# Query projections as pairs of high and low tokens in the two cross attentions of a fused two-block kernel, and four convolution taps in another place

## The reference

```
q = (h @ xq_w).reshape(B, S, 4, 256)                 # h is the normed stream
s = einsum('bshd,bmhd->bhsm', q, k) * 256 ** -0.5
o = einsum('bhsm,bmhd->bshd', softmax(s), v).reshape(B, S, 1024)
x = x + o @ xo_w
...
u = a * sigmoid(b)
y = conv_general_dilated(u, conv_w[:, None, :], padding=[(30, 0)], feature_group_count=512) + conv_b
```

## Time and profile before

| | |
|---|---|
| median of 3 runs | 913.3 us (912.95 to 915.75) |
| time of the profiled execution | 913.01 us |
| its span, first to last instruction | 910.9 us |
| mean granted TensorE clock | 0.999 |
| PE busy | 901.4 us, 99% |
| DVE busy | 661.6 us, 73% |
| ACT busy | 504.2 us, 55% |
| HBM read | 162.65 MB, 180 GB/s over the span |

### The profile page before, as it was taken

The page is one execution under the profiler, slowest core; times in us unless marked ns, Lnnn a source line. Parts: engine busy times, 40 slices in busy tenths (PEclk is TensorE's granted clock), DMA queues, the critical chain, the costliest instruction groups (busy, mean ns, idle before and its releaser), DMA issues.

```text
span 910.9 us, 12836 instructions
## 1 busy us (share of the span) xinstructions
PE 901.4 (99%) x5160; PEld 787.4 (86%) x5160; DVE 661.6 (73%) x920; ACT 504.2 (55%) x584; POOL 24.3 (3%) x69
## 2 busy tenths in 40 slices
PE   9999999999999999999999999999999999999997
PEld 8888998889888888888888988888899888888886
DVE  5799999987577666656967996646686676565665
ACT  6796435655555444445656757744464654544444
POOL 1600010000000000000000000000000000000000
PEclk9999999999999999999999999999999999999999
DMA  9746555454355666654755455455453456666551
GB/s 353 253 159 223 183 199 185 139 185 140 92 186 186 195 199 197 190 185 153 238 188 183 159 166 183 152 175 187 173 185 103 144 183 191 196 193 197 189 185 47
DMA packets 101280, 164.38 MB, mean 180 GB/s; under 512 B 2736, under 2 KB 71088, under 8 KB 101104
## 3 DMA queue, kind: packets, MB, share of 16 engines
q1 hardware_dynamic: 100528, 161.71, 54.2%
q0 software_dynamic: 560, 1.84, 0.7%
q10 hardware_dynamic: 144, 0.16, 0.1%
HBM read 162.65 MB, written 1.05 MB: 180 GB/s over the span
## 4 chain that ended last, share of the span: by engine, by line
PE 92%; DVE 5%; DMA 2%; ACT 1%; issue 1%; SPq 0%; DVEq 0%; ACTq 0%
PE ps L609 20%; PE ps L611 19%; PE ps L610 19%; PE ps L646 18%; PE ps L650 9%; DVE w_lo L1719 1%; DVE c_acc L1865 1%; DMA w_ring<-in_w_in 1%; PE ps L737 1%; DMA head_raw<-in_head 1%; PE ps L857 0%; ACT w_hi L1227 0%; PE ps L774 0%; DVE mem_l L1734 0%; PE ps L826 0%
## 5 line engine op out<-in xcount | busy, mean ns | idle before, releaser
L1719 DVE TENSOR_TENSOR w_lo<-w_ring,w_hi 128x2048 fp32r<-128x2048 f32 x146 | 333.4, 2288 | 114.2 <-ACT w_hi L1227 113.2
L1227 ACT ACTIVATE w_hi<-w_ring 128x2048 fp32r<-128x2048 f32 x146 | 278.6, 1911 | 88.3 <-DMA w_ring<-in_w_in 27.3
L646 PE MATMUL ps<-xx,w_hi 128*128 128x512 f32 x720 | 171.8, 391 | 0.3
L646 PEld LDWEIGHTS ps<-xx,w_hi 128*128 128x128 f32 x720 | 133.3, 188 | 27.4 <-issue 0.7
L609 PE MATMUL ps<-w_hi,xx 128*128 128x512 f32 x304 | 120.2, 395 | 0.0
L611 PE MATMUL ps<-w_hi,xx 128*128 128x512 f32 x304 | 118.6, 390 | 0.0
L610 PE MATMUL ps<-w_lo,xx 128*128 128x512 f32 x304 | 118.5, 390 | 0.0
L650 PEld LDWEIGHTS ps<-xx,w_lo 128*128 128x128 f32 x720 | 92.3, 191 | 3.5
L650 PE MATMUL ps<-xx,w_lo 128*128 128x256 f32 x720 | 93.4, 283 | 0.0
L609 PE MATMUL ps<-w_hi,ff_h 128*128 128x512 f32 (+1 forms) x218 | 84.7, 389 | 0.0
L610 PE MATMUL ps<-w_lo,ff_h 128*128 128x512 f32 (+1 forms) x218 | 84.6, 388 | 0.0
(11 more groups left out here) (339 smaller groups left out, 1335.9 us busy)
## 6 DMA issues: line engine op xcount, KB each, us to landing
w_ring<-in_w_in SPq DMA_DIRECT2D x34, 1024.0 KB, 5.1
w_ring<-in_mlp_up_w SPq DMA_DIRECT2D x16, 1024.0 KB, 5.6
w_ring<-in_mlp_down_w SPq DMA_DIRECT2D x16, 1024.0 KB, 4.9
w_ring<-in_w_gate_ffn SPq DMA_DIRECT2D x11, 1024.0 KB, 5.3
w_ring<-in_w_up_ffn SPq DMA_DIRECT2D x11, 1024.0 KB, 5.3
w_ring<-in_w_down_ffn SPq DMA_DIRECT2D x11, 1024.0 KB, 4.9
w_ring<-in_xkv_w SPq DMA_DIRECT2D x8, 1024.0 KB, 5.4
w_ring<-in_w_out SPq DMA_DIRECT2D x8, 1024.0 KB, 4.8
```

The source lines that it names most:

```text
L646: pe.matmul(feat(bank + b), wh[:, k, b * P:(b + 1) * P], xx[:, k, :, :].rearrange("p e t -> p (e t)"), start=k == 0, stop=False)
L1227: act.activation(w_hi[:, s, :], w_ring[:, s, :], ACT.Copy).then_inc(hi_done, 1)
L1719: dve.tensor_tensor(w_lo[:, s, :], w_ring[:, s, :], w_hi[:, s, :].bitcast(F32), ALU.subtract).then_inc(lo_done, 1)
```

## The change

In each attention the second and the third query slab (heads 1 and 2) are taken by `form_a_pair` in place of `form_a`: head 1 into banks 6 and 7, head 2 into banks 4 and 5. The fourth stays with `form_a` but goes into `feat(2)`, the first stays as it is. A new tile `q_s` (in the place of a part of `xn`) takes the sums: ACT copies the low tokens' halves there (`q_half`), DVE adds the high tokens' halves (`q_sum`), and only then `q(j)` and `q_lo(j)` read it. On ACT `q_half(1)` stands ahead of `q(1)` and `q_half(2)` ahead of `q(2)`. On DVE `q_sum(1)` takes the place of `q_lo(1)`, which moves behind `normalise(0)`; `q_sum(2)` stands ahead of `q_lo(2)`. The banks in which head 0, 1, 2 and 3 are turned and their values formed are `feat(3)`, `feat(0)`, `feat(1)` and `feat(2)` (`place`). In the convolution four of the 16 steps ahead of `lo(11)` move behind it, so that 8 stand between `lo(11)` and `lo(12)` in place of 4.

```diff
+        q_s = at("q_s", [P, 2, 2, S], xn0)
+        pair_banks = {1: ps[:, 6:8, :], 2: ps[:, 4:6, :]}
+        xq_half, xq_sum = sem("xq_half"), sem("xq_sum")
...
             def form_a_pair(i, bank, step=0, ready=(), low_ready=None):
+                banks = bank if type(bank) is tuple else (4 + bank, 5 + bank)
...
             def x_attention(b, i_q, i_o, ready, between):        # PE
+                place = (3, 0, 1, 2)
...
                 form_a(i_q, (0,), (xh, xl), 256, 0, *ready)
-                form_a(i_q + 1, (1,), (xh, xl))
+                form_a_pair(i_q + 1, 2)
                 scores(0)
-                form_a(i_q + 2, (2,), (xh, xl))
+                form_a_pair(i_q + 2, 0)
                 scores(1)
                 turn(0)
-                form_a(i_q + 3, (3,), (xh, xl))
+                form_a(i_q + 3, (2,), (xh, xl))
                 scores(2)
...
             def x_attention(b, i_q, i_o):                        # ACT
                 def q(j):
+                    if j in (1, 2):
+                        act.wait_ge(xq_sum, 2 * b + j)
+                        src = q_s[:, j - 1, :, :]
+                    else:
+                        used_slab(i_q + j)
+                        src = blocks(feat(2 if j else 0))
+                    act.activation(q_h[:, 2 * j:2 * j + 2, :], src, ACT.Copy).then_inc(xq_hi, 1)
+
+                def q_half(j):
+                    act.wait_ge(norm_sq, 2 * (Q_XA, Q_XA2)[b] + 2)
                     used_slab(i_q + j)
-                    act.activation(q_h[:, 2 * j:2 * j + 2, :], blocks(feat(j)), ACT.Copy).then_inc(xq_hi, 1)
+                    act.activation(q_s[:, j - 1, :, :], pair_banks[j][:, :, S:2 * S], ACT.Copy).then_inc(xq_half, 1)
...
                 q(0)
+                q_half(1)
                 q(1)
                 hi(i_o)
                 exps(0)
                 hi(i_o + 1)
+                q_half(2)
                 q(2)
                 p_t(0)
...
-            conv(16)
+            conv(12)
...
             lo(11)
-            conv(4)
+            conv(8)
             lo(12)
...
+                def q_sum(j):                                    # DVE
+                    dve.wait_ge(xq_half, 2 * b + j)
+                    q = q_s[:, j - 1, :, :]
+                    dve.tensor_tensor(q, pair_banks[j][:, :, 0:S], q, ALU.add).then_inc(xq_sum, 1)
...
                 q_lo(0)
                 if b == 0:
                     lo(I_Q1 + 3)
-                q_lo(1)
+                q_sum(1)
                 maxima(0)
                 normalise(0)
+                q_lo(1)
                 lo(i_o)
                 lo(i_o + 1)
+                q_sum(2)
                 q_lo(2)
                 p_lo(0)
```

More of the change, by code:

```diff
@@ L645, in form_a_pair @@
                     for b in range(2):
-                        pe.matmul(feat(bank + b), wh[:, k, b * P:(b + 1) * P], xx[:, k, :, :].rearrange("p e t -> p (e t)"), start=k == 0, stop=False)
+                        pe.matmul(ps[:, banks[b], :], wh[:, k, b * P:(b + 1) * P], xx[:, k, :, :].rearrange("p e t -> p (e t)"), start=k == 0, stop=False)
                 pe.wait_ge(lo_done, weight_count(i) + step)
@@ L649, in form_a_pair @@
                     for k in range(KD):
-                        mm = pe.matmul(feat(bank + b)[:, 0:S], wl[:, k, b * P:(b + 1) * P], xx[:, k, 0, :], start=False, stop=k == KD - 1)
+                        mm = pe.matmul(ps[:, banks[b], 0:S], wl[:, k, b * P:(b + 1) * P], xx[:, k, 0, :], start=False, stop=k == KD - 1)
                 mm.then_inc(slab_used, 1)
@@ L773, in turn @@
                         for m in range(2):
-                            mm = pe.transpose(feat(hd)[:, m * S + tb * P:m * S + (tb + 1) * P],
+                            mm = pe.transpose(feat(place[hd])[:, m * S + tb * P:m * S + (tb + 1) * P],
                                               prob[:, u % 4, m * P:(m + 1) * P], ident[:, :])
@@ L783, in values @@
                         for m in range(2):
-                            mm = mm3(feat(hd)[:, kk * S:(kk + 1) * S], [v[:, m, f * P:(f + 1) * P] for v in v_split[b]],
+                            mm = mm3(feat(place[hd])[:, kk * S:(kk + 1) * S], [v[:, m, f * P:(f + 1) * P] for v in v_split[b]],
                                      [p[:, hd % 2, m, :] for p in (probT_h, probT_l)], m == 0, m == 1)
@@ L1433, in p_t @@
                         act.wait_ge(xo_ready, 4 * b + hd - 1)
-                    act.activation(probT_h[:, hd % 2, :, :], blocks(feat(hd)), ACT.Copy).then_inc(xp_hi, 1)
+                    act.activation(probT_h[:, hd % 2, :, :], blocks(feat(place[hd])), ACT.Copy).then_inc(xp_hi, 1)
                 def out_hi(hd):
                     act.wait_ge(xo_ready, 4 * b + hd + 1)
-                    act.activation(xh[:, 2 * hd:2 * hd + 2, :], blocks(feat(hd)), ACT.Copy).then_inc(xo_hi, 1)
+                    act.activation(xh[:, 2 * hd:2 * hd + 2, :], blocks(feat(place[hd])), ACT.Copy).then_inc(xo_hi, 1)
                 q(0)
+                q_half(1)
                 q(1)
@@ L2022, in out_lo @@
                     f = slice(2 * hd, 2 * hd + 2)
-                    dve.tensor_tensor(xl[:, f, :], blocks(feat(hd)), xh[:, f, :].bitcast(F32), ALU.subtract).then_inc(xo_lo, 1)
+                    dve.tensor_tensor(xl[:, f, :], blocks(feat(place[hd])), xh[:, f, :].bitcast(F32), ALU.subtract).then_inc(xo_lo, 1)
+                place = (3, 0, 1, 2)
+                def q_sum(j):
+                    dve.wait_ge(xq_half, 2 * b + j)
+                    q = q_s[:, j - 1, :, :]
+                    dve.tensor_tensor(q, pair_banks[j][:, :, 0:S], q, ALU.add).then_inc(xq_sum, 1)
                 def q_lo(j):
@@ L2027, in q_lo @@
                     f = slice(2 * j, 2 * j + 2)
-                    dve.tensor_tensor(q_l[:, f, :], blocks(feat(j)), q_h[:, f, :].bitcast(F32), ALU.subtract).then_inc(xq_ready, 1)
+                    q = q_s[:, j - 1, :, :] if j in (1, 2) else blocks(feat(2 if j else 0))
+                    dve.tensor_tensor(q_l[:, f, :], q, q_h[:, f, :].bitcast(F32), ALU.subtract).then_inc(xq_ready, 1)
                 def p_lo(hd):
                     dve.wait_ge(xp_hi, 4 * b + hd + 1)
-                    dve.tensor_tensor(probT_l[:, hd % 2, :, :], blocks(feat(hd)), probT_h[:, hd % 2, :, :].bitcast(F32), ALU.subtract).then_inc(xpT_ready, 1)
+                    dve.tensor_tensor(probT_l[:, hd % 2, :, :], blocks(feat(place[hd])), probT_h[:, hd % 2, :, :].bitcast(F32), ALU.subtract).then_inc(xpT_ready, 1)
                 q_lo(0)
```

## The result

The changed kernel takes 916.4 us (median of 15, 915.2 to 918.2) against 913.6 for the kernel before (median of 15: 14 lie at 912.8 to 915.8, one stray execution took 1817.8); the ratio is 1.003, 95% interval 1.0023 to 1.0037. So it is 2.7 us slower, right at the bound of 0.3%. The prediction had 915.3 and a range of 912.5 to 917.0; it gave 0.78 to a difference within 0.3% and 0.19 to slower. The profiled execution took 915.28 us with a span of 913.3, 2.4 more than before; the forecast span was 912.9.

What follows compares the result with a forecast made beforehand. PE was taken to bound the kernel, DVE the stretch of the taps. First attention +1.70, second +0.29 and taps 0 gave +1.99 us on 913.01, so 915.0; with 0.3 for the median 915.3 us, range 912.5 to 917.0.

Steps and rivals of the forecast that it cites:

- The pairs: Attention query slabs: a pair slab takes 5.57 us against 5.76, sparing 0.19 on PE; four make 0.76 if usable.
- The chain to `scores(1)`: First attention: q(1) waits for q_sum(1), delaying exps(0) and q_lo(1); PE stands still 1.89 us, scores(1) 1.70 late.
- The rival that hides the chains: Both attentions: ACT and DVE chains hidden, pairs pay -0.19 each; 912.3 to 912.9 us with taps' gain; chance 0.14.
- Second attention: Same chain there: q(1) 1.18 us late, scores(1) at 679.60 against 679.31, +0.29 us.
- The first attention: Whole first attention: loss at scores(1), with the second sum hidden by the fourth slab; +1.70 us.
- The taps: Convolution: PE gains 0.64 us at slab 11, lost again before L914 because DVE bounds the stretch; 0 us.
- The second wait at `scores(2)`: Rival, first attention: q_sum(2) late behind two low parts, PE waits again; 916.2 us, up to 917; chance 0.11.
- The clock: Rival: clock falls after the 1.89 us wait, one slab at half speed costs 5.76 us; up to 921; chance 0.04.
- A rule on the clock: Step: full clock after the last matmul at the kernel's end, so no fall of the clock enters the sum.

Runs made afterwards that it cites:

- act_order: Changed kernel with ACT's hi(i_o) moved ahead of q(1) in the attentions; 913.70 us against 913.67 for the kernel before, ratio 0.9999.
- q_lo_early: Changed kernel with DVE's q_lo(1) moved ahead of normalise(0), behind maxima(0); 913.78 us against 913.83 for the kernel before, ratio 1.0.
- taps_alone: Kernel before with only the four convolution taps moved, attentions untouched; 913.56 us against 913.83, ratio 0.9999.
- two_waits: Changed kernel with two unread DVE additions ahead of q_lo(1) in the second attention, lengthening PE's wait there; 918.47 us against 914.17 for the kernel before.
- longer_wait: Changed kernel with two unread DVE additions ahead of q_lo(1) in the first attention, lengthening PE's wait; 920.05 us against 913.67 for the kernel before.
- best2: Changed kernel with hi(i_o) ahead of q(1) on ACT, q_lo(1) before normalise(0) and query low parts later on DVE; 912.29 us against 913.67 before.
- mid_wait: Changed kernel with one unread DVE addition ahead of q_lo(1) in the first attention; PE idle there for 3.2 us, median 918.61 us.
- whole_again: The changed kernel unaltered, run once more on another chip; 916.73 us against 913.98 for the kernel before.
- filled_again: Changed kernel with 14 unread matmuls filling PE's wait before scores(1) in the first attention; 916.05 us against 913.98 for the kernel before.

## Why the prediction came out as it did

**The pairs.** Right: 5.57 us a slab in place of 5.76, and nothing of it arrives. The first pair's gain ends at `q_lo(0)` (`scores(0)` at 205.95, forecast 205.97), the second's in the new wait.

**The chain to `scores(1)`.** Right link by link: `q(1)` at 208.73 (208.76), `exps(0)` at 212.48 (212.51), `q_lo(1)` at 214.19 (214.21), `scores(1)` at 214.92 (214.96). act_order and q_lo_early each cut one link and each takes the loss away. The rival that hides the chains failed where it was said to, at `q(1)` behind the sum.

**Second attention.** Right in kind, short in size: the forecast had +0.29, the traces have +0.53 (from the transposes of the stream ahead of it, 1.78 us late, to those behind it, 2.31 late), with 0.34 of it at `scores(1)`, 0.08 ahead of `scores(0)` and 0.11 behind `scores(1)`. The first attention cost 1.76 against 1.70, up to the first slab of the MLP. These two are 0.30 of the 0.34 us between the measured 2.33 and the forecast 1.99; the other 0.04 arose between the attentions and was not looked for.

**The taps.** Right in the sum, which was 0, and in its reason, that DVE is the bound; wrong in the place. The forecast had 0.7 to 0.8 us of idle time before L914, the trace has 0.35: the earlier PE first ran into the low part of slab 15 and stood there for 0.41 us. taps_alone shows both again.

**The second wait at `scores(2)`.** It did not come: `q_lo(2)` started at 220.57, and there was as much cover as worked out.

**The clock.** Mis-sized. "A rule on the clock" put no fall into the sum and gave it a chance of 0.04, since a longer stretch without matmuls at the end of the kernel had been followed by full clock. One execution's row is no bound for others: the clock did fall behind a wait of 2.1 us in two_waits, of 4.4 us in longer_wait and of 2.0 us at the start in best2. The rule of the Trainium skill, page TensorE: Matmul & The Clock Gate, section Why this matters for your kernels, that an idle gap can throw the array back to the lower clock, holds for these three (granted clock 0.50 behind each). The price was overstated in turn: 1.5 us in two_waits and 2.4 in longer_wait, not up to a slab's 5.76. What it does to the unaltered change is not shown, as no profile has a fall behind its wait.

**The distance to the median.** From the forecast 915.3 to the measured 916.37 there are three parts. The kernel before has a median of 913.63 over 15 executions where the forecast started from 913.3 over three: 0.33 us. The changed stretch costs 0.34 more than the sum, as above. The last 0.4 is in the spread: without the five executions at 0.996 or 0.997 the median of the changed kernel is 915.75. But about a quarter of the executions of the kernel before are such too, and the median execution itself (916.37) reports 0.999. So the chain, which was worked out right, put the number inside the range; how much of the last 0.4 us is a fall behind the wait stays open.

## What to carry to other kernels

A step that adds a link between two engines (copy half, add half, then go on) is paid for by everything queued behind the waiting step, not by its own 0.6 us: put independent work, here the next high part, between the two ends of the link before the form is judged. Where PE has no slack, write the queues of the engines side by side with durations of the trace; four starting times came out within 0.04 us that way. And a wait of PE by two microseconds or more should be priced with a possible fall of the clock on top; one profile with full clock does not rule it out, and the times and clocks of many executions should be read beside it.

## What the runs showed of the hardware that was not expected

The granted clock fell to half behind waits of PE that other executions, or another place in the same execution, took without harm (in one execution of two_waits 1.9 us without and 2.1 us with a fall; at the start 2.0 us with it in best2 and 2.1 us without in taps_alone; 3.2 us without in mid_wait's profile). Where it fell, it stayed down while PE was already working again, for a few microseconds, and cost 1.5 us in two_waits and 2.4 in longer_wait. About a quarter of the executions of the kernel before are some 2 us late; the four profiles with a fall at 8 to 16 us (best2, whole_again, filled_again, two_waits) reach the first attention late by as much.
